# Loads of the down weights issued by ScalarE's queue in place of SyncE's, in a transformer layer on one Trainium2 core

## What is computed

```python
def reference(x, ...):
    h = x
    h = h + gla_mixer(rmsnorm(h, norm_mix_g[0]), ...)
    h = h + swiglu_ffn(rmsnorm(h, norm_ffn_g[0]), ffn_w_gu[0], ffn_w_down[0])
    return rmsnorm(h, final_norm_g)

def swiglu_ffn(h, w_gu, w_down):
    g, u = jnp.split(h @ w_gu, 2, axis=-1)
    return (jax.nn.silu(g) * u) @ w_down
```

## Time and profile before

| what | value |
|---|---|
| time, median of 3 runs | 2280.22 us (2276.13 to 2283.58) |
| time of the profiled execution | 2280.23 us |
| its span, first to last instruction | 2278.5 us |
| TensorE busy (matmuls) | 2171.3 us, 95% of the span |
| GpSimd, VectorE, ScalarE busy | 71%, 60%, 36% |
| granted TensorE clock, mean | 0.982 of full speed |
| DMA q1 (SyncE) | 366.73 MB, 45.3% of 16 engines' span |
| DMA q10 (ScalarE) | 32.05 MB, 4.3% |
| w_raw<-in_ffn_w_down, issue to landing, median | 4.4 us |
| hid<-hop (1 MB), issue to landing, median | 9.5 us |

### The profile page before, as it was taken

How to read it: one execution, slowest core, us unless ns; L and a number is a source line. 1 busy time by engine, 2 the same in 40 slices (tenths; PEclk the granted TensorE clock), 3 DMA queues, 4 the chain that set the end, 5 groups by cost and what they waited for, 6 DMA issues and landing times.

```text
span 2278.5 us, 27753 instructions
## 1 busy us (share of the span) xinstructions
PE 2171.3 (95%) x9912; PEld 1794.7 (79%) x9912; DVE 1358.2 (60%) x1775; ACT 823.4 (36%) x1444; POOL 1616.7 (71%) x1294
## 2 busy tenths in 40 slices
PE   6999999899989999879999998999999999999998
PEld 4888788778877888668888887788888878778876
DVE  5345544554555444266757574675757567877787
ACT  4224333433333333244444442444444422132223
POOL 5555666566645675658888886888888886868784
PEclk8999999999999999999999999999999999999999
DMA  4322354325522655574343439443434578748773
GB/s 126 110 84 65 114 171 141 111 90 176 160 102 75 203 167 179 183 258 166 136 169 134 171 132 360 174 168 137 166 139 166 199 283 329 269 175 352 269 306 118
DMA packets 223689, 400.55 MB, mean 176 GB/s; under 512 B 16864, under 2 KB 156128, under 8 KB 214592
## 3 DMA queue, kind: packets, MB, share of 16 engines
q1 hardware_dynamic: 191696, 366.73, 45.3%
q10 hardware_dynamic: 31856, 32.05, 4.3%
HBM read 271.85 MB, written 126.88 MB: 175 GB/s over the span
## 4 chain that ended last, share of the span: by engine, by line
PE 69%; POOL 11%; DVE 6%; DMA 5%; ACT 4%; SPq 2%; issue 2%; ACTq 0%; POOLq 0%; DVEq 0%
PE ps L678 22%; PE ps L680 21%; PE ps L679 21%; POOL w_op L622 6%; PE ps L708 1%; DMA w_raw<-in_ffn_w_down 1%; PE ps L792 1%; POOL ring_lo L613 1%; DVE xs L1394 1%; SPq L435 1%; DMA xop<-x_stage 1%; ACT junk L993 1%; POOL w_raw L640 1%; DVE lc L1422 1%; POOL w_raw L632 1%
## 5 line engine op out<-in xcount | busy, mean ns | idle before, releaser
L622 POOL TENSOR_TENSOR w_op<-w_raw,w_op 128x512 fp32r<-128x512 f32 x330 | 478.5, 1462 | 123.0 <-ACT w_op L983 119.9
L678 PE MATMUL ps<-x_op,w_op 128*128 128x512 f32 x1232 | 483.9, 393 | 19.6 <-issue 10.2
L680 PE MATMUL ps<-x_op,w_op 128*128 128x512 f32 x1232 | 482.8, 392 | 0.0
L679 PE MATMUL ps<-x_op,w_op 128*128 128x512 f32 x1232 | 482.4, 392 | 0.0
L610 POOL TENSOR_SCALAR ring_hi<-raw 128x512 fp32r<-128x512 f32 x256 | 176.2, 688 | 341.8 <-issue 165.7
L613 POOL TENSOR_TENSOR ring_lo<-raw,ring_hi 128x512 fp32r<-128x512 f32 x256 | 349.2, 1364 | 21.4
L983 ACT ACTIVATE w_op<-w_raw 128x512 fp32r<-128x512 f32 x330 | 202.7, 626 | 367.4 <-POOL w_raw L640 146.9
L678 PEld LDWEIGHTS ps<-x_op,w_op 128*128 128x128 f32 x1232 | 233.2, 189 | 72.0 <-issue 24.2
L680 PEld LDWEIGHTS ps<-x_op,w_op 128*128 128x128 f32 x1232 | 232.9, 189 | 49.0
L679 PEld LDWEIGHTS ps<-x_op,w_op 128*128 128x128 f32 x1232 | 233.2, 189 | 48.0
L678 PE MATMUL ps<-w_op,hid 128*128 128x512 f32 x616 | 243.7, 396 | 13.6 <-DVE acc L1803 8.6
(11 more groups left out here) (184 smaller groups left out, 3965.8 us busy)
## 6 DMA issues: line engine op xcount, KB each, us to landing
hop<-stage SPq DMA_DIRECT2D x154, 512.0 KB, 2.9
hid<-hop SPq DMA_DIRECT2D x70, 1024.0 KB, 9.5
raw<-in_gla_w_in SPq DMA_DIRECT2D x192, 256.0 KB, 3.2
w_raw<-in_ffn_w_gu SPq DMA_DIRECT2D x176, 256.0 KB, 3.9
xop<-x_stage ACTq DMA_DIRECT2D x56, 512.0 KB, 3.7
x_op<-xop SPq DMA_DIRECT2D x56, 512.0 KB, 11.4
w_raw<-in_ffn_w_down SPq DMA_DIRECT2D x88, 256.0 KB, 4.4
raw<-in_gla_w_out SPq DMA_DIRECT2D x64, 256.0 KB, 3.1
```

What stands on the lines that cost most here:

```text
L622: pool.tensor_tensor(shaped(q, tile[:, 1, :]), source(q, i), shaped(q, tile[:, 0, :]).bitcast(F32), ALU.subtract).then_inc(op_ready[i], 1)
L678: pe.matmul(out, l_hi, r_hi, start=first, stop=False, skip_group_check=more)
L679: pe.matmul(out, l_hi, r_lo, start=False, stop=False, skip_group_check=more)
L680: return pe.matmul(out, l_lo, r_hi, start=False, stop=last, skip_group_check=more)
```

## The change

SyncE no longer loads the quads of slices 2 to 11. ScalarE gets its own `load_quad`, with the same wait and the same four DMAs, and issues the quads of slice n + 1 after its splits of slice n. Quads of slices 0 and 1 stay with SyncE, as does everything else.

```diff
--- before.py
+++ after.py
@@ -525,9 +525,6 @@
             load_quad(U_QUADS + 1)
             for n, part in enumerate(slices):
                 B = part["B"]
-                if n > 1:
-                    for q in part["quads"]:
-                        load_quad(q)
                 if part["part"] == 0:
                     granules = 7 * NP * (B + 1)
                     for slot in range(4):
@@ -1310,6 +1307,12 @@
             pair = U_QUADS // 2 - 1
             hidden_hi(pair, 3)
 
+            def load_quad(q):
+
+                act.wait_ge(op_ready[6], q - 1)
+                for dst, src in raw_parts(q):
+                    act.dma_start(dst, src).then_inc(w_loaded[q % 2], 16)
+
             def square_of(B, j, number):
 
                 done, out_half, th = ((u3_done, 1, 1), (c11_done, 0, 0), (c21_done, 0, 1), (c12_done, 1, 0))[number]
@@ -1348,6 +1351,9 @@
                         hidden_hi(U_QUADS // 2 - 1, 5 if i == 0 else 6)
                     if before["part"] == LAST_SLICE and j == len(slices[n]["quads"]) - 1 and i in (3, 4, 5, 6):
                         square_of(0, 3, i - 3)
+                if n + 1 < len(slices):
+                    for q in slices[n + 1]["quads"]:
+                        load_quad(q)
                 if before["part"] == LAST_SLICE:
                     root_of(0, 2)
                     root_of(0, 3)
```

## The result

The changed kernel takes 2311.32 us (median of 4 runs, 2307.53 to 2313.34), the kernel before beside it 2279.12 us. The ratio is 1.0138, 95% interval 1.0115 to 1.0161: **slower by 32 us**. The forecast was 2319, its range 2279 to 2332.

What follows compares the result with a forecast made beforehand. Mostly TensorE's matmuls, with GpSimd's serial load-and-split loop holding TensorE up at the last slice. Each half 13 + 2.5 + 2.5 + 1.5 = 19.5 us, both 39, on 2280: 2319 us, range 2279 to 2332.

Steps and rivals of the forecast that it cites:

- The path: Load and split of slices 3 to 5 and 9 to 11 form one serial loop, without slack at the last slice.
- The mechanism: Weights and hid on two hardware queues share the DMA engines one packet each in turn, whatever its size; chance 0.62.
- The 13: Slices 3 and 9: the second weight quad lands late behind hid packets, +13 us each, bounds +0.3 and +18.
- The 2.5: Slices 4, 5, 10 and 11: one hid load falls into the quads' transfer, +2.5 us each, bounds 0 and 5.
- The clock: Last slice of each half: TensorE restarts at a lower clock after its wait, +1.5 us, bounds 0 and 2.5.
- Slice 7, costed at nothing as "hidden": Loads of slices 2, 7 and 8 get slower by 1 to 3 us, hidden by GpSimd's wait for operands: 0.
- VectorE's gain at nothing: Earlier hid cures the late ht, worth 2.75 us on VectorE; costed at nothing because TensorE then waits longer for GpSimd.
- no wait of VectorE for ht: Sign in the profile after: VectorE no longer waits for ht loads anywhere.
- the other signs: Landings above 10 us at slices 3, 9; 5 to 8 at 4, 5, 10, 11; TensorE's GpSimd wait 20 to 40.
- The milder rival: Engines give both queues equal time, not equal packets: +3.2 us at slice 3, 2292 us in all; chance 0.16.
- Nothing changes: Weight transfers keep their time because hid seldom collides; TensorE's 3 us back become longer GpSimd waits: 2281 us; chance 0.11.
- faster: The burst was the harm: ht in time, weight landings toward 3 us at six places, 2272 us; chance 0.11.

Runs made afterwards that it cites:

- the parts: Changed kernel with slices 3 and 9 back on SyncE's queue: 2291.96 us; kernel before with only slices 3 and 9 on ScalarE's queue: 2295.76 us.

## Why the prediction was right, and where its sizes were off

**The path** was right. Load and split of slices 3 to 5 and 9 to 11 are one serial loop without slack; delay put there came out at the end (13 + 17 for the parts, 32 for the whole), and holding hid back until the weights had landed took all of it away.

**The mechanism** was right: the queues take turns by packets, nearly one each, 294 to 356 and with 4 KB rows 266 to 274. It is not exactly one: without the small packets under 512 B the first pair is 265 of hid beside 323 of weights. The Trainium skill (DMA: Bandwidth & Descriptors, "Queues, rings and completion order") has round robin at packet granularity between rows of a DMA engine; the traces come near to it in four mixes of packet sizes (573 to 591 in the earlier trace rows, 294 to 356, 266 to 274 and 199 to 172). The Trainium skill also says (same page, "Issuing engines are not separate DMA queues") that issuing from more engines saves only issue time. The runs in which hid is held back agree with it, 2277 and 2271 us on either queue; the change as it stood lost 32 us, since it also gave up an order inside one queue.

**The terms**, each taken from the end of the step before to the start of w_t3b, where the prediction's delay was to appear. In slices 3 to 5 the marks are 1905.63 or the first ACTq issue, and w_t3b's start, of the chain above; before, w_t3b started at 1919.35, 1954.02 and 1990.29, 11.53, 10.45 and 10.77 us behind its mark. In slices 9 to 11 w_t3b starts 20.58, 11.84 and 15.08 us behind its mark, before 11.43, 11.03 and 11.06.

| term | predicted | slices 3, 4, 5 | slices 9, 10, 11 |
|---|---|---|---|
| second quad of slice 3 / 9 | +13 | 20.96 - 11.53 = +9.4 | +9.2 |
| slice 4 / 10 | +2.5 | 16.75 - 10.45 = +6.3 | +0.8 |
| slice 5 / 11 | +2.5 | +1.9 | +4.0 |
| GpSimd's steps between them | 0 | -3.1 | -1.6 |
| sum, with the clock apart | +18 | +14.5 | +12.4 |

- *The 13* was too large by 4. The step that failed is mainly the first quad, which I had landing near 1919, 11.2 us behind the mark. ScalarE's first split of it starts at 1914.39, 8.8 us behind, where it had landed after 7.4 before: hid had slowed it by little. The step was also reckoned wrong: at its own 314 GB/s some 184 packets would be through by 1912.4, not 270, and the first quad would have come out later still. The second quad then took 12.1 us more, to 1926.5, close to the 11.8 of the packets and not far from the 13.2 taken.
- *The 2.5* hangs on whether TensorE's freeing of a hid tile falls into the load: +6.3, +1.9, +0.8, +4.0, mean 3.3. As a mean the estimate held, for a single slice it said little. The reading that the freed tile decides it was not tested. SyncE's four hid loads of slice 4 begin at 1940.51, not at 1932.5 as predicted, so they stand nearer to the weights of 1949.26.
- *GpSimd's steps* between these marks took 67.2 us in the first half, where they had taken 70.4, and 68.3 for 69.9 in the second. The prediction had no term for it, and its cause was not tried.
- *The clock* was costed at 1.5 us a half. After a stall of 8.16 us the granted clock at the start of the last slice was 0.50, the level of 1.2 GHz, for 5 us, with 12 matmuls started where 22 do at 0.23 us each:

```profile
2023.30:2028.30 5.00, 5.00 (x12) 3.94 (x13) 0.69 (x1) 0.00 (x0) 4.85 (x4) 0.50 0.06 6
```

  12 x (0.43 - 0.23) = 2.4 us. The stretch behind the second half's path was longer by 2.2 us, so the term should have been about 2.3.
- *Slice 7, costed at nothing as "hidden"*, was the real miss: a term put at nothing. Beside its loads four of hid, one of ht and three output stores were issued; the second quad landed after 18.56 us, and in the window of 2104 to 2111 us TensorE started 12 matmuls where 30 fit at 0.23 us: some 4 us lost, 2.9 of them in a wait for GpSimd and the rest at the lower clock. The chain and the window:

```profile
2082.32 18.56 DMA w_raw<-in_ffn_w_down
...
2100.95 1.31 POOL w_t3b L627
```

```profile
2104.00:2111.00 7.00, 4.07 (x12) 2.93 (x11) 1.21 (x2) 3.75 (x7) 7.00 (x6) 0.76 0.99 334
```

  I had argued cover from slice 8, where GpSimd waits 3.63 us for operands; slice 7 has two quads and its own cover, which I did not read.
- *VectorE's gain at nothing* held in the sum: TensorE's wait for VectorE fell from 8.6 to 2.4 us, and the time didn't come back. The late ht of slice 4 did go, as predicted: VectorE's 2.75 us at 1964.15 is gone, and an ht load takes 7.7 us to landing, 10.7 before (medians). What VectorE still waits for ht, 4.0 us in all, lies in slice 1, where it had waited 1.41 us before:

```profile
1882.04 1.23 DVE L1828 TENSOR_TENSOR acc<-acc,ht 128x1024 f32<-128x1024 f32 x1 [2.65 <-DMA ht<-hres]
...
1887.14 1.23 DVE L1828 TENSOR_TENSOR acc<-acc,ht 128x1024 f32<-128x1024 f32 x1 [1.36 <-DMA ht<-hres]
```

  So the sign "no wait of VectorE for ht" was put too widely. Of the other signs, the landings of slices 3 and 9 (15.87 and 15.55 us) and TensorE's 34.9 us for GpSimd came as said. It waited seven times, not two to four, the landings at slices 4, 5, 10 and 11 spread from 4.37 to 11.32 us, not 5 to 8, and GpSimd's idle time for slice 3's weights was 5.5 + 8.0 = 13.5 us, not 17.

39 us predicted, 32.8 measured: the two 13s were 7.4 too large, the four 2.5s 3.0 too small, GpSimd's steps gave 4.7, slice 7 and the clock together (5.9 + 2.2 for 3) took 5.1 more, and the earlier start gave 2.2; in sum -6.2. So the nearness of the forecast is partly luck, since the misses of the sizes cancel in part. The milder rival (2292) falls by the shares of the engines' time, 75.3% to 25.6% where it needs equal ones. "Nothing changes" and "faster" fall by the landings: the shortest of the moved loads takes 2.7 us as before, but the median went from 4.7 to 6.8 and the longest from 10.6 to 18.6.

## What to carry to other kernels

A queue is also an order: before a load is moved from one queue to another, ask what stood behind it, for that is what it will share the DMA engines with. Where two queues were full here they took turns by packets, nearly one each, so a load that is on the path and has the smaller packets gets the smaller share of bytes (2 KB beside 8 KB: 0.66 of 2.84 MB); keep it ahead on the same queue, or hold the other back until it has landed, and give it long rows. Cost the places called hidden from their own rows, each one.

## What the runs showed of the hardware that I had not expected

- Rows of 4 KB in place of 2 KB moved weights at 401 in place of 353 GB/s on one queue (two stretches of 3 us), and 0.45% of the kernel's time hung on it: 2271.24 us, with 2270.83 on ScalarE's queue the fastest versions here.
- DMAs of 64 partitions with 4 KB rows were slow alone and bad neighbours. Alone they moved 246 GB/s, where 128 partitions and the same rows moved 401. Beside hid the engines fell to 298 GB/s, from 421. A 4 KB packet of the weights held an engine 0.287 x 112 / 172 = 187 ns against 0.356 x 112 / 274 = 146 ns, and the 8 KB packets of hid beside it 0.727 x 112 / 199 = 409 ns against 276. Why was not tried.
- The time to issue the same eight DMAs on ScalarE's queue varied from 3.72 to 6.54 us, on SyncE's before from 3.65 to 4.62; a single issue took up to 1.67 us. Busy DMA engines don't explain it: they were 81% busy in the slowest case, at slice 4, and fully busy in the fastest, at slice 7. The cause is open.

```profile
1949.26 6.54 ACTq L1314 DMA_DIRECT2D w_raw<-in_ffn_w_down  x8
...
2079.05 3.72 ACTq L1314 DMA_DIRECT2D w_raw<-in_ffn_w_down  x8
```
- Waits added to SyncE to restore its old pace made the change twice as bad (2346 us): both queues are let go by one event, and the weight loads of slices 3 to 5 took 15.62, 18.81 and 18.19 us.
